# Three edits to a one-core hybrid block kernel: the order of the last expert's down products, the form of the block ends, and two small products of the mLSTM stage

## What the kernel computes

```python
# mLSTM, per head: scores weighted, then the weighted sum and its norm
s = jnp.einsum('bhld,bhsd->bhls', qt, kt) * dw
num = jnp.einsum('bhls,bhsd->bhld', s, vt) + ...
den = jnp.sum(s, axis=-1) + ...
h = num / jnp.maximum(jnp.abs(den), jnp.exp(-m_row))[..., None]
...
# experts
h = lax.ragged_dot(xs, w_gate_up, group_sizes) + b_gate_up[e_sorted]
gate, up = h[:, :D_FF], h[:, D_FF:]
gate = jnp.minimum(gate, SWIGLU_LIMIT)
up = jnp.clip(up, -SWIGLU_LIMIT, SWIGLU_LIMIT)
a = (up + 1.0) * (gate * jax.nn.sigmoid(SWIGLU_ALPHA * gate))
y = lax.ragged_dot(a, w_down, group_sizes) + b_down[e_sorted]
```

## Time and profile before

| | |
|---|---|
| time, median of 3 runs | 2308.63 us (2306.97 to 2308.93) |
| the profiled execution's own time | 2305.04 us |
| its span, first to last instruction | 2303.3 us |
| TensorE busy | 2224.2 us, 97% |
| TensorE weight load busy (beside the matmuls) | 1788.9 us, 78% |
| VectorE busy | 1575.2 us, 68% |
| ScalarE busy | 1304.1 us, 57% |
| GpSimd busy | 303.2 us, 13% |
| mean granted TensorE clock | 0.976 of full |

### The profile page before, as it was taken

How to read it: one execution, slowest core, us unless ns; L and a number is a source line. 1 busy time by engine, 2 the same in 40 slices (tenths; PEclk the granted TensorE clock), 3 DMA queues, 4 the chain that set the end, 5 groups by cost and what they waited for, 6 DMA issues and landing times.

```text
span 2303.3 us, 30249 instructions
## 1 busy us (share of the span) xinstructions
PE 2224.2 (97%) x10196; PEld 1788.9 (78%) x10196; DVE 1575.2 (68%) x1693; ACT 1304.1 (57%) x1528; POOL 303.2 (13%) x401
## 2 busy tenths in 40 slices
PE   6999899899999999999799999999999999999997
PEld 5888677566667888888578888888888888888885
DVE  5777345543444334335598889888898898888984
ACT  5656443234223433223277777777777777777773
POOL 3334100201231000001010110101101111011010
PEclk8999999999999999999699999999999999999999
DMA  4110333220112333334599999999999999999992
GB/s 181 56 55 28 119 110 108 74 62 31 46 37 92 100 128 137 93 99 150 227 346 368 370 360 373 364 368 358 368 370 370 361 362 369 366 369 365 369 363 84
DMA packets 89011, 515.71 MB, mean 224 GB/s; under 512 B 15108, under 2 KB 16132, under 8 KB 38184
## 3 DMA queue, kind: packets, MB, share of 16 engines
q1 hardware_dynamic: 79448, 498.05, 58.2%
q0 software_dynamic: 9216, 16.81, 3.0%
q10 hardware_dynamic: 288, 0.09, 0.0%
HBM read 508.59 MB, written 23.33 MB: 231 GB/s over the span
## 4 chain that ended last, share of the span: by engine, by line
PE 50%; DVE 1%; ACT 0%; issue 0%; POOL 0%; POOLq 0%; DVEq 0%; ACTq 0%
PE bank L2120 15%; PE bank L2122 15%; PE bank L2121 15%; PE bank L2141 1%; PE bank L2131 1%; PE bank L2172 1%; PE bank L2156 0%; DVE moe_lo L2111 0%; ACT moe_hi L2104 0%; DVE moe_a L2218 0%; DVE moe_um L2212 0%; DVE moe_XTl L2196 0%; POOL out L2270 0%; ACT moe_XTh L2190 0%; DVE moe_aTl L2232 0%
## 5 line engine op out<-in xcount | busy, mean ns | idle before, releaser
L2111 DVE TENSOR_TENSOR moe_lo<-moe_raw,moe_hi 128x2048 fp32r<-128x2048 f32 x382 | 854.8, 2284 | 18.9 <-ACT moe_hi L2104 15.5
L2104 ACT ACTIVATE moe_hi<-moe_raw 128x2048 fp32r<-128x2048 f32 x380 | 728.5, 1919 | 169.5 <-PE bank L2122 162.2
L2120 PE MATMUL bank<-moe_hi,moe_XTh 128*128 128x512 f32 x1024 | 404.4, 395 | 0.0
L2121 PE MATMUL bank<-moe_lo,moe_XTh 128*128 128x512 f32 x1024 | 404.0, 395 | 0.0
L2122 PE MATMUL bank<-moe_hi,moe_XTl 128*128 128x512 f32 x1024 | 403.7, 394 | 0.0
L168 ACT ACTIVATE unit_hi<-unit_raw 128x1024 fp32r<-128x1024 f32 x116 | 122.3, 1059 | 241.5 <-DMA unit_raw<-in_w_units 235.4
L174 DVE TENSOR_TENSOR unit_lo<-unit_raw,unit_hi 128x1024 fp32r<-128x1024 f32 x116 | 145.3, 1258 | 157.2 <-ACT unit_hi L168 156.7
L2122 PEld LDWEIGHTS bank<-moe_hi,moe_XTl 128*128 128x128 f32 x1024 | 193.4, 189 | 44.6
L2121 PEld LDWEIGHTS bank<-moe_lo,moe_XTh 128*128 128x128 f32 x1024 | 193.4, 189 | 44.3
L2120 PEld LDWEIGHTS bank<-moe_hi,moe_XTh 128*128 128x128 f32 x1024 | 193.9, 189 | 40.3
L2120 PE MATMUL bank<-moe_hi,moe_aTh 128*128 128x512 f32 x512 | 200.2, 391 | 1.4 <-DVE moe_aTl L2232 1.4
(11 more groups left out here) (358 smaller groups left out, 3668.0 us busy)
## 6 DMA issues: line engine op xcount, KB each, us to landing
moe_raw<-in_w_moe SPq DMA_DIRECT2D x384, 1024.0 KB, 7.0
unit_raw<-in_w_units SPq DMA_DIRECT2D x116, 512.0 KB, 3.5
da_slab<-in_w_qkv SPq DMA_DIRECT2D x8, 1536.0 KB, 6.6
x_sb<-in_x SPq DMA_DIRECT2D x4, 512.0 KB, 5.5
yda_d<-y_daT SPq DMA_DIRECT2D x1, 2048.0 KB, 6.3
y_daT<-in_blocks_qk SPq DMA_DIRECT2D x1, 2048.0 KB, 11.6
y_daT<-yda_d SPq DMA_DIRECT2D x1, 2048.0 KB, 8.0
y_daT<-in_x SPq DMA_DIRECT2D x1, 2048.0 KB, 8.7
```

Of the source, the lines that this page charges most:

```text
L2104: nc.scalar.activation(HI[ring(n, pos)][:], RAW[pos][:], ACT.Copy).then_inc(s_hi, 1)
L2111: nc.vector.tensor_tensor(LO[pos][:], RAW[pos][:], HI[ring(n, pos)][:].bitcast(F32), ALU.subtract).then_inc(s_lo, 1)
L2120: nc.tensor.matmul(bank[:], xh[:, x], HI[ring][:, w], start=start and k == 0, stop=False)
L2121: nc.tensor.matmul(bank[:], xh[:, x], LO[pos][:, w], start=False, stop=False)
```

## The change

1. Every block is opened with `no_gpsimd_drain=True`: GpSimd has no drain at a block's end, and the barrier there is made of semaphores alone. The barrier in `forget_sems` (L131) is made of semaphores alone as well (`sem_only=True`).
2. In the ml stage two of the four key chunks of head 1 are put behind head 0's weighted sum.
3. The last expert's down products are done in the order 6, 4, 7, 5 (both first depth halves, then both second ones). Unit 6 is ahead of the last turning, the others behind it. High and low parts are made in the order 6, 7, 4, 5: the high parts of 6 and 7 in slots 9 and 10 of the last turn, the low parts of both ahead of SwiGLU. Output half 1 is weighed before half 0.

```diff
     def forget_sems(self):
         self.nc.clear_and_free_semaphores(self.sems)
-        self.nc.all_engine_barrier()
+        self.nc.all_engine_barrier(sem_only=True)
...
-    with nc.Block() as block:
+    with nc.Block(no_gpsimd_drain=True) as block:
...
-            def kq(h):
-                for c in range(CT):
+            def kq(h, c0=0, c1=CT):
+                for c in range(c0, c1):
...
-            kq(1)
+            kq(1, 0, 2)
             weigh(0)
+            kq(1, 2, CT)
             z(0, 3)
...
+    LAST = (6, 7, 4, 5)
...
         if isinstance(n, int) and n == NE:
-            return 12 * NE + pos - 3
+            return 12 * NE + LAST.index(pos) + 1
...
-        elif not (isinstance(n, int) and n == NE and pos >= 6):
+        elif isinstance(n, int) and n == NE:
+            act.wait_ge(s_use, count(n - 1, pos if pos >= 6 else pos + 6))
+        else:
             act.wait_ge(s_use, count(n, pos - 6) if pos >= 6 else count(n - 1, pos + 6))
...
# TensorE, behind the last turn
-            turn_a(pe, NE - 1, 1)
-            down(pe, NE - 1, NE, [(count(NE, p), p, p % 6) for p in DOWN])
+            pe.wait_ge(s_XTl, NE)
+            pe.wait_ge(s_aTl, START + 2 * NE - 1)
+            last = lambda p, half: unit(pe, count(NE, p), p, p % 6, Yb[p // 6], aTh, aTl, 4 * half, half == 0, half == 1)
+            last(6, 0)
+            turn_a(pe, NE - 1, 1)
+            last(4, 0)
+            pe.wait_ge(s_aTl, START + 2 * NE)
+            last(7, 1)
+            last(5, 1)
...
# ScalarE, in ahead()
+                elif isinstance(n, int) and n == NE - 1:
+                    if slot in (9, 10):
+                        hi(act, NE, slot - 3)
...
# ScalarE, behind the last turn
+            hi(act, NE, 4)
             hi(act, NE, 5)
             keep_a_hi(act, NE - 1, 1, NE * 12 - 4)
-            for pos in (6, 7):
-                hi(act, NE, pos)
-            weigh(act, NE - 1, 0, count(NE, 5))
-            weigh(act, NE - 1, 1, count(NE, 7))
+            weigh(act, NE - 1, 1, 12 * NE + 3)
+            weigh(act, NE - 1, 0, 12 * NE + 4)
...
# VectorE, behind the last turn
-            lo(dve, NE, 4)
-            swiglu(dve, NE - 1, 1, NE * 12)
-            keep_a_lo(dve, NE - 1, 1)
-            for pos in (5, 6, 7):
-                lo(dve, NE, pos)
+            lo(dve, NE, 6)
+            lo(dve, NE, 7)
+            swiglu(dve, NE - 1, 1, NE * 12)
+            lo(dve, NE, 4)
+            keep_a_lo(dve, NE - 1, 1)
+            lo(dve, NE, 5)
```

More of the change, by code:

```diff
@@ L2237, in weigh @@
         act.wait_ge(s_use, ready)
-        if j == 0:
+        if j == (1 if isinstance(n, int) and n == NE - 1 else 0):
             act.wait_ge(s_LS, n + 1)
```

## The result

| | before | after |
|---|---|---|
| median of 5 runs (lowest to highest), us | 2307.8 (2305.5 to 2308.93) | 2294.68 (2293.48 to 2296.42) |
| profiled execution: its time, its span, us | 2305.04, 2303.3 | 2293.95, 2292.0 |
| outside the span, us | 1.74 | 1.95 |
| mean granted clock of TensorE | 0.976 | 0.977 |

The changed kernel is faster: the ratio is 0.9945, with a 95% interval from 0.9931 to 0.996. The forecast was 2298.1 with a range from 2295.3 to 2303.0. The profiled execution fell by 11.1, the medians by 13.1 (the ratio gives 12.7, with an interval from 9.2 to 15.9), and the forecast said 10.5. The median of 2308.63, from which the forecast was counted, is that of three of the five runs before.

The account below looks back on a forecast made before the run. TensorE, busy 97% of the span, was taken as the bound, so gains come from its idle time and slow matmuls. 5.4 + 2.5 + 1.2 + 0.1 + 1.3 = 10.5 us below 2308.63 gave 2298.1, range 2295.3 to 2303.

Parts of the forecast that it names:

- last expert: End of the last expert: the new order lets the last down matmul start near 2287.0 instead of 2292.38, 5.4 us saved.
- last drain: Program end: without GpSimd's drain the final barrier closes 2.5 us earlier, from 0 to 2.6.
- mix to moe: Block end between mix and moe: without GpSimd's drain TensorE starts 1.2 us earlier, from 0 to 1.3.
- key chunks: Head 0 of the mLSTM stage: TensorE's wait for the normed rows before the turning goes, 1.3 us, from 0 to 1.5.
- The term of 0.1 for the barriers: Barriers of `forget_sems`: GpSimd's drain of 40 to 46 ns goes three times, 0.1 us.
- The drains' time comes back elsewhere: Rival: the removed drains' time returns in the clearing after mix or outside the span, 2.5 to 3.7 us; chance 0.18.
- VectorE late: Rival: in the tail one more low part is late and TensorE waits up to 2.3 us again, 2300.4; chance 0.10.
- No effect: Rival: the drains come back and only unit 6 is hidden in the tail, gain 4.2 us, 2304.4; chance 0.07.
- slower by the clock: Rival: the clock stays low for one whole expert after the moe stage's changed start, costing 29.6 us, 2327.7; chance 0.05.

Follow-up runs that it names:

- e2: The kernel before with only the two key chunks moved behind head 0's weighted sum; 2306.02 us, ratio 1.0001.
- e3: The kernel before with only the new order in the last expert; 2299.66 us, ratio 0.997.
- e9: The changed kernel with GpSimd's drain at the end of the last block kept; 2298.4 us, ratio 0.9967 to the kernel before.
- e7: The changed kernel with the ml stage's four small loads issued ahead of the 2 MB key and query blocks; 2287.95 us, ratio 0.9924 to the kernel before.
- e10: The kernel before with only the ml stage's four small loads issued ahead of the key and query blocks; 2298.12 us, ratio 0.9967.
- e8: The changed kernel with e7's load order and unit 4's high part made ahead of unit 7's, in another ring place; 2285.85 us, ratio 0.991 to the kernel before.
- e5: The changed kernel with the last turning of `a` put back ahead of unit 6; 2295.15 us, ratio 0.9949 to the kernel before.

## Why the prediction missed its range

The steps of the sum, against the first pair of traces and over all traces that have the old or the new form of the place, with their number:

| term | forecast | first pair | old form, all | new form, all |
|---|---|---|---|---|
| last expert | 5.4 | 17.57 to 12.15: 5.42 | 17.49 to 18.88 (5) | 12.14 to 12.17 (5) |
| last drain | 2.5 | 8.94 to 6.66: 2.28 | 8.83 to 9.22 (6) | 6.39 to 6.66 (7) |
| mix to moe | 1.2 | 5.78 to 4.69: 1.09 | 5.71 to 5.90 (5) | 4.31 to 4.69 (8) |
| the whole mix stage, to that turning | | 392.39 to 390.96: 1.43 | 391.90 to 392.56 (5) | 390.63 to 391.12 (8) |
| key chunks | 1.3 | 21.38 to 19.85: 1.53 | 21.03 to 21.38 (5) | 19.84 or 21.5 (8) |
| mLSTM stage's start to that turning, old order of loads | | 188.1 to 185.5: 2.6 | 187.5 to 188.1 (4) | 185.1 to 187.5 (6) |

The four were to give 10.4 and gave 5.42 + 2.28 + 1.09 + 1.53 = 10.32 in the profiled pair. By the averages over all the traces in the table they are 5.7, 2.5, 1.3 and 0.6, together about 10. The steps inside them held too: TensorE goes straight into unit 6, waits once for unit 4's low part (0.5, forecast 0.7), and the clock stays at 1.00. The term of 0.1 for the barriers was too small to be read. The key chunks are the term that holds least: their 1.5 stands in four traces of eight, and in the other four a low stretch of the clock takes it all (21.5). Over the whole way from the stage's start, with the old order of loads, the averages differ by 1.7, but the wait for the gate weights is part of that way.

**The drains' time comes back elsewhere** fell. The end is 2.28 shorter and the time outside the span only 0.2 to 0.3 longer, in kernels with and without the last drain. (The Trainium skill, "Runtime: NRT & Kernel Launch", section "The launch sequence", places a resetting of the DMA rings of about 2 us behind the kernel; no growth of 2 is there.) **VectorE late** fell: one wait of 0.51. **No effect** and **slower by the clock** fell as well; the low stretch at the changed restart cost nothing more than before, 32.04 from the first expert's first turning to its second, and 31.70 before. But its premise, that the low level follows on idle stretches and lasts 3.1 to some 5 us, holds only in part: behind the idle stretches of e2's tail thirteen matmuls were slow, 5.8 us, and in head 0 it came without one.

**The step that failed** is "The median of the runs is 3.6 above the profiled one, at 2308.63, and 10.5 below it is 2298.1". It started the sum from a wrong place. The forecast lies 3.4 above the measured 2294.68. Of that, 2.3 is the start: the median of three runs, 2308.63, was taken as the middle of the kernel, and lies 2.3 above the median of 69. Another 1.5 is gain, 12.0 by all runs against 10.5, and 0.4 goes the other way, since the five runs' 2294.68 lies above the ten's 2294.31. The distance from a profiled execution to its kernel's median is no property of the kernel: 3.6 by the three runs, 1.3 by all 69, and 0.4 for the changed kernel (2293.95 to 2294.31). From 2306.3 the same sum gives 2295.8, 1.1 above the measured time, and the range would have begun at 2293.0 instead of 2295.3, so the measured time would have lain inside it. The 1 us that the range allowed for the medians was worked out from three runs that happened to lie within 2 us, where 69 lie within 11.3.

What the 1.5 is made of is settled only in part. The profiled pair, where the spans differ by 11.3, has 1.0 beyond the four terms. The mLSTM stage's first unit matmul starts 0.27 later; TensorE's wait ahead of it is 2.5 in all eight traces with the new block end there and 2.1 in all five with the old, a cost of the block ends that the forecast put at nothing. The wait for the gate weights is 2.1 shorter, and about half of that is given back before head 0, whose key chunks come 0.8 earlier. The old tail holds a low stretch that was at its short end in the profile (17.57; the mean of five is 17.8). e3, which has only the tail, lost 6.9 by its runs, with an interval from 4.8 to 9.0. That the wait for the gate weights is shorter on average with the new block ends (5.2 in six traces, 5.9 in four) is within its own spread, so I don't count it as shown. Resampling the 69 and the 10 runs gives an interval of about 10.1 to 12.9 for the difference of the medians and of 10.6 to 12.3 for that of the means; the forecast's 10.5 lies at the lower edge of both. So a little more gain than the terms give is likely, its place stays open, and no single term is shown to be mis-sized.

Four expectations of times were missed, none beyond its interval: e9 (some 4 instead of 2.3), where the trace has a low stretch in a place that the edit does not touch, and e7, e10 and e8 (6.4 instead of 3 to 5, 7.6 instead of 6, 8.5 instead of 3.5 to 5.5), where the price of the wait left out the slow matmuls behind it. The same omission was avoided in the forecast's tail, where the 1.5 of the low level is in the 5.4.

## What to carry to other kernels

Cost a change place by place against the profiled execution, and forecast the time from the middle of as many runs as there are; with three of them, the range needs the spread of single runs (here a standard deviation of 2.1 us) beside the bounds of the terms. When an A/B result looks a little too large or too small, compare the intervals between landmarks that no edit touches before looking for a missing term. A wait that changes between two traces without an edit near it is worth an experiment of its own: here moving one line gave 6 to 8 us, and the slow matmuls behind it belong to its price.

## What was not expected of the hardware

The granted clock fell to the lower level, 1.2 GHz, at places that differ between executions. In the two stretches from 45 to 60 above, the same idle time of 3.12 brought the low level in one trace and not in the other. In head 0 there is no idle time at all ahead of the fall: the new order took 19.84 in four traces and 21.5 in four others, and TensorE's records fill the time without a gap in both kinds. (The 20 matmuls of the denominator, of one column each, are among them, from 562.1 on.) The same stretch in the changed kernel, then in e5, each with an earlier stretch of 5 us:

```profile
560.00:565.00 5.00, 5.00 (x31) 3.75 (x31) 1.01 (x4) 1.27 (x3) 4.29 (x6) 1.00 0.00 0
566.00:568.00 2.00, 2.00 (x6) 0.94 (x5) 1.97 (x3) 0.00 (x0) 0.00 (x0) 1.00 0.00 0
```

```profile
560.00:565.00 5.00, 5.00 (x33) 3.81 (x32) 1.01 (x4) 1.34 (x3) 4.15 (x7) 1.00 0.00 0
566.00:568.00 2.00, 2.00 (x3) 0.68 (x2) 1.74 (x2) 0.00 (x0) 0.00 (x0) 0.50 0.00 0
```

It cost 21.52 - 19.85 = 1.7 there. In the two of those four traces that have the old order of loads, the way ahead of it, from the end of the wait for the gate weights, is shorter than in the four that took 19.84 (138.2 and 138.3 in e5 and e9, 139.0 to 139.6), so part of it may be a low stretch that came later. In the expert loop, in contrast, the way from the second turning to the last is 1080.26 to 1080.28 in all 13 traces, at clock 1.00. So in these traces what spreads the runs of this kernel (a standard deviation of 2.1 us before) lies ahead of that way and in the old tail, and the new tail, at clock 1.00, has taken one such place away.

The landing of the 8 KB `sel` load behind the 2 MB load varied as well: from its issue to GpSimd's start it was 12.2 before and 9.8 after, and between 9.2 and 12.2 over the ten traces with the same loads in the same order. Issued ahead of the 2 MB it was 5.2 to 6.4 (three traces).
